# adaLN columns by TensorE with the weights stationary, all of x ahead of the second part, and q and k of a unit in turn

## The reference

```python
cond = jax.nn.silu(c)                                    # (1, 1024)
for i in range(2):
    shift, scale, gate = jnp.split(cond @ w_ada[i] + b_ada[i], 3, axis=-1)
    h = rms_norm(x, g_pre[i]) * (1.0 + scale) + shift    # (1024, 1024)
    u = h @ w_in[i]                                      # q, k, v and z, 1024 columns each
    y = attention_i(u[..., :3072])                       # diff: lambda from exp of two dot products
    y = (y * jax.nn.silu(u[..., 3072:])) @ w_out[i]
    x = x + gate * rms_norm(y, g_post[i])
```

## Time and profile before

| | |
|---|---|
| median of 3 runs | 1553.56 us (1552.69 to 1553.84) |
| the profiled execution | 1552.89 us |
| its span, first to last instruction | 1551.0 us |
| PE busy | 1382.5 us, 89% |
| DVE, ACT, POOL busy | 1057.0, 879.3, 554.8 us |
| mean granted TensorE clock | 0.962 |
| first score matmul of the first layer | at 101.63 us |
| first matmul of z's projection behind it | at 102.15 us |

### The profile page before, as it was taken

The page is one execution under the profiler, slowest core; times in us unless marked ns, Lnnn a source line. Parts: engine busy times, 40 slices in busy tenths (PEclk is TensorE's granted clock), DMA queues, the critical chain, the costliest instruction groups (busy, mean ns, idle before and its releaser), DMA issues. The chain is left out here.

```text
span 1551.0 us, 23600 instructions
## 1 busy us (share of the span) xinstructions
PE 1382.5 (89%) x7154; PEld 1138.9 (73%) x7154; DVE 1057.0 (68%) x1824; ACT 879.3 (57%) x1712; POOL 554.8 (36%) x325
## 2 busy tenths in 40 slices
PE   4688999999999999986997899999999999995898
PEld 2567777777777777775875678887877888784776
DVE  4868888797979797978457656556565656557415
ACT  4346555565656565555445467667676757667322
POOL 1024555555646564636222322121122212122204
PEclk9899999999999999996998899999999999996999
DMA  9012111102021111122034001100100010002014
GB/s 342 28 41 64 46 54 52 56 27 80 28 68 41 54 54 54 54 73 90 1 112 146 28 28 32 37 27 27 41 27 27 27 39 28 27 14 109 0 58 174
DMA packets 112649, 89.82 MB, mean 58 GB/s; under 512 B 2553, under 2 KB 101090, under 8 KB 112610
## 3 DMA queue, kind: packets, MB, share of 16 engines
q1 hardware_dynamic: 112320, 89.15, 18.3%
q10 hardware_dynamic: 290, 0.18, 0.1%
HBM read 80.92 MB, written 8.40 MB: 58 GB/s over the span
## 5 line engine op out<-in xcount | busy, mean ns | idle before, releaser
L674 PE MATMUL bank<-h_hi,w_hi 128*128 128x512 f32 x976 | 396.0, 406 | 9.1 <-POOL h_lo L583 4.5
L674 PE MATMUL bank<-h_lo,w_hi 128*128 128x512 f32 x976 | 393.2, 403 | 0.0
L674 PE MATMUL bank<-h_hi,w_lo 128*128 128x512 f32 x976 | 390.7, 400 | 0.0
L644 POOL TENSOR_TENSOR w_lo<-w_raw,w_hi 128x1024 fp32r<-128x1024 f32 x59 | 159.4, 2701 | 374.6 <-ACT w_hi L638 374.5
L1288 POOL TENSOR_TENSOR a<-a,stick 128x128 f32<-128x128 f32 (+7 forms) x128 | 189.6, 1486 | 251.0 <-DVE stick L1153 251.0
L1153 DVE TENSOR_TENSOR_SCAN stick<-b 128x128 f32<-128x128 f32 (+7 forms) x128 | 204.1, 1594 | 41.4 <-ACT b L1057 41.4
L674 PEld LDWEIGHTS bank<-h_hi,w_hi 128*128 128x128 f32 x976 | 185.9, 190 | 41.6 <-issue 10.0
L674 PEld LDWEIGHTS bank<-h_hi,w_lo 128*128 128x128 f32 x976 | 185.5, 190 | 33.1
L674 PEld LDWEIGHTS bank<-h_lo,w_hi 128*128 128x128 f32 x976 | 185.5, 190 | 30.4
L1056 ACT ACTIVATE a<-bank 128x512 f32<-128x512 f32 (+2 forms) x192 | 94.7, 493 | 90.5 <-PE bank L960 52.6
L1069 ACT ACTIVATE wt_hi<-bank 128x512 fp32r<-128x512 f32 (+2 forms) x192 | 87.8, 494 | 74.8 <-PE bank L976 73.0
(11 more groups left out here) (215 smaller groups left out, 3036.8 us busy)
## 6 DMA issues: line engine op xcount, KB each, us to landing
w_raw<-in_w_in_dram SPq DMA_DIRECT2D x63, 512.0 KB, 4.0
ada_piece<-in_w_ada_dram SPq DMA_DIRECT2D x32, 512.0 KB, 3.8
p_ada<-in_w_ada_dram SPq DMA_DIRECT2D x8, 1024.0 KB, 13.2
wo_raw<-in_w_out_dram SPq DMA_DIRECT2D x8, 1024.0 KB, 9.9
p_x<-in_x_dram SPq DMA_DIRECT2D x8, 512.0 KB, 7.7
o_x<-in_x_dram SPq DMA_DIRECT2D x8, 512.0 KB, 4.1
x_between<-o_res SPq DMA_DIRECT2D x8, 512.0 KB, 2.9
o_x<-x_between SPq DMA_DIRECT2D x8, 512.0 KB, 4.1
```

Source lines behind the costliest of these rows:

```text
L644: self.nc.gpsimd.tensor_tensor(self.m["w_lo"][s][:, :, :], self.m["w_raw"][s][:, :, :], self.m["w_hi"][s][:, :, :].bitcast(F32), ALU.subtr ...
L674: mm = nc.tensor.matmul(self.bank[half][:, :], w[:, k, :], h[:, k, half * HALF:(half + 1) * HALF], start=(i == 0), stop=(i == GROUP - 1))
```

## The change

Parts 0 to 3 are all made by one form on TensorE: for each of 8 blocks of the condition and each of 4 column blocks a matmul with the 128x128 block of w_ada stationary and the condition's column moving, summed in PSUM straight to columns, 32 float32 matmuls a part. The row product, its copy, `accumulate` and the matmuls with ones leave. All eight tiles are normalised and turned before part 1; part 0 stands on TensorE between turns 2 and 3. The tiles' PSUM banks go round in three pairs. Phases 0 and 1 are made in a row, and q and k are projected unit by unit in turn, in phase 2 for the first four of its eight units. Columns 2 and 3 stand where they stood, between v's phases 0 and 1 and phase 2. The loads are ordered accordingly. GpSimd's w_lo is made in four pieces a weight. The Exp of lambda and the three small VectorE instructions on it move to the second layer's start; the loading of the Sigmoid table moves ahead of the last copies. ScalarE's split of z's weights moves behind all six copies of q and k, and VectorE packs one half of q before it takes k.

```diff
-    T = ((0, 1), (6, 7), (0, 1), (6, 7), (6, 7), (4, 1), (6, 7), (4, 1))
+    T = ((0, 1), (6, 7), (3, 4))
...
# sync
         for h in range(2):
             ada(0, h)
-        ada(1, 0)
-        weights(0, self.proj.loaded[0])
-        ada(1, 1)
-        weights(1, self.proj.loaded[1])
         for t in range(4, NT):
             tile(t)
+        weights(0, self.proj.loaded[0])
+        for h in range(2):
+            ada(1, h)
+        weights(1, self.proj.loaded[1])
         weights(2, self.v_loaded)
...
# gpsimd
-            nc.gpsimd.tensor_tensor(self.w_lo[kind][:, :, :], self.w_raw[kind][:, :, :],
-                                    self.w_hi[kind][:, :, :].bitcast(F32), ALU.subtract).then_inc(self.proj.lo_done, 1)
+            for k in range(0, KT, 2):
+                ins = nc.gpsimd.tensor_tensor(self.w_lo[kind][:, k:k + 2, :], self.w_raw[kind][:, k:k + 2, :],
+                                              self.w_hi[kind][:, k:k + 2, :].bitcast(F32), ALU.subtract)
+            ins.then_inc(self.proj.lo_done, 1)
...
# scalar
-        act.wait_ge(self.lam_sum, 2)
-        nc.scalar.activation(self.lam_sums[:, 2:4], self.lam_sums[:, 0:2], ACT.Exp).then_inc(self.lam_exp, 1)
...
+        for t in range(NT):
+            square(t)
+            root(t)
             if t:
                 keep_left(t - 1)
...
+            if t == NT - 1:
+                act.preload_act_table_set("sigmoid_and_others")
+                weights_hi(0, self.proj.loaded[0])
+        keep_left(NT - 1)
         weights_hi(1, self.proj.loaded[1])
...
# vector
+        for t in range(NT):
             normalise(t)
             if t:
                 keep_right(t - 1)
-        keep_right(3)
-        accumulate(1)
+        keep_right(NT - 1)
         columns(0)
...
         modulate(1)
-        accumulate(2)
-        accumulate(3)
         columns(1)
         modulate(2)
...
# tensor
         def columns(i):
             at = (0, KT, self.LOW, KT + self.LOW)[i]
...
+            for k in range(KT):
+                if k % self.LOW == 0:
+                    pe.wait_ge(self.ada_in[i][k // self.LOW], 16)
+                for j in range(self.LOW):
+                    mm = nc.tensor.matmul(self.cols[:, at + j:at + j + 1], self.ada_w[i][:, k, j * P:(j + 1) * P],
+                                          m["cond"][:, k:k + 1], start=(k == 0 and j == 0),
+                                          stop=(k == KT - 1 and j == self.LOW - 1))
+            mm.then_inc(self.cols_done, 1)
...
+        for t in range(NT):
             turn(t)
+            if t == 2:
+                pe.wait_ge(self.cond_done, 1)
+                columns(0)
+        columns(1)
         pe.wait_ge(self.left_kept, NT)
         pe.wait_ge(self.right_kept, NT)
-        for kind in range(2):
-            project(kind, 1)
-        pe.wait_ge(self.proj.lo_done, done(2))
-        project(2, 0)
-        project(2, 1)
-        for i in range(2, 4):
-            columns(i).then_inc(self.cols_done, 1)
+        for phase in range(2):
+            project((0, 1), phase, range(self.LOW))
+        for phase in range(2):
+            project((2,), phase, range(self.LOW))
+        columns(2)
+        columns(3)
+        project((0, 1), 2, range(self.LOW))
         for kind in range(3):
-            project(kind, 2)
+            project((kind,), 2, range(0 if kind == 2 else self.LOW, KT))
...
# behind the prologue: scalar, then vector
             for n in range(6):
                 pack_hi(0, n)
-                if n == 3:
-                    proj.split_hi(act, 0, 3)
+            proj.split_hi(act, 0, 3)
...
-            for n in range(4):
-                pack.lo(dve, 0, n)
+                for n in ((0,), (2, 3, 1))[kind]:
+                    pack.lo(dve, 0, n)
...
# second layer, vector
+            dve.wait_ge(pro.lam_exp, 1)
+            nc.vector.tensor_tensor(lam[:, 0:1], lam[:, 7:8], lam[:, 6:7], ALU.subtract).then_inc(table, 1)
+            dve.wait_ge(table, 5)
+            nc.vector.tensor_scalar(lam[:, 2:3], lam[:, 0:1], -lam_init, None, ALU.add).then_inc(table, 1)
+            nc.vector.tensor_scalar(lam[:, 3:4], lam[:, 1:2], 1.0 - lam_init, None, ALU.mult).then_inc(table, 1)
+            dve.wait_ge(table, 7)
```

More of the change, by code:

```diff
@@ L211, in __init__ @@
         self.vec = m["ada_sum"]
-        self.vec_t, self.row = m["pm"][2], m["pm"][5]
+        self.vec_t = m["pm"][2]
         self.cols = m["pm"][2][:, P:P + 2 * KT]
@@ L311, in statistics, with root @@
                                  accum_out=st[:, 4 * t:4 * t + 1]).then_inc(self.squares, 1)
+        def root(t):
             act.wait_ge(self.mean_done, t + 1)
@@ L378, in keep_right @@
             dve.wait_ge(self.turned, t + 1)
-            t4 = m["pm"][self.T[t][1]][:, :].rearrange("p (k t) -> p k t", t=P)
+            t4 = m["pm"][self.T[t % 3][1]][:, :].rearrange("p (k t) -> p k t", t=P)
             nc.vector.tensor_copy(m["y"][:, 4:8, t * P:(t + 1) * P], t4).then_inc(self.right_kept, 1)
[L382 to L398, removed]
         def columns(batch):
@@ L438, in vector @@
                                            accum_out=self.lam_sums[:, j:j + 1]).then_inc(self.lam_sum, 1)
-        for t in range(4):
+        for t in range(NT):
             normalise(t)
@@ L442, in vector @@
                 keep_right(t - 1)
-        keep_right(3)
-        accumulate(1)
+        keep_right(NT - 1)
         columns(0)
[L446 to L453, removed]
         dve.wait_ge(self.left_kept, NT)
         dve.wait_ge(self.right_kept, NT)
+        modulate(0)
         modulate(1)
-        accumulate(2)
-        accumulate(3)
         columns(1)
         modulate(2)
[L461 to L464, removed]
+        for r in range(2):
+            nc.vector.memset(m["stick"][r][:, S:S + 1], 1.0).then_inc(self.one_set, 1)
     def tensor(self, pe):
@@ L480, in columns @@
             at = (0, KT, self.LOW, KT + self.LOW)[i]
[L481 to L491, removed]
@@ L492, in columns @@
-            return mm
-        def project(kind, phase):
-            units, first = self.units(phase)
[L496 to L506, removed]
+            for k in range(KT):
[5 more added lines that the diff above has]
+                                          stop=(k == KT - 1 and j == self.LOW - 1))
@@ new lines, in columns, with project @@
+            mm.then_inc(self.cols_done, 1)
+        def project(kinds, phase, picked):
+            units, first = self.units(phase)
+            for n in picked:
+                k, half = units[n]
+                pe.wait_ge(self.hi_done, first + n + 1)
+                pe.wait_ge(self.lo_done, first + n + 1)
+                for kind in kinds:
+                    if phase == 0 and n == 0:
+                        pe.wait_ge(self.proj.lo_done, done(kind))
+                    for part in range(MULS):
+                        w = (self.w_hi, self.w_hi, self.w_lo)[part][kind]
+                        h = (m["h_hi"], m["h_lo"], m["h_hi"])[part]
+                        mm = nc.tensor.matmul(m["pm"][self.ACC[kind][half]][:, :], w[:, k, :],
+                                              h[:, k, half * HALF:(half + 1) * HALF],
+                                              start=(k == 0 and part == 0), stop=(k == KT - 1 and part == MULS - 1))
+                    if k == KT - 1:
+                        mm.then_inc(self.proj.group_done, 1)
@@ L1143, in _ @@
             pro.vector(dve)
-            for r in range(2):
-                nc.vector.memset(m["stick"][r][:, S:S + 1], 1.0).then_inc(one_set, 1)
             def scan(p, t):
@@ L1599, in _ @@
             act.preload_act_table_set("natural_log_exp_and_others")
+            act.wait_ge(pro.lam_sum, 2)
+            nc.scalar.activation(m["lam"][:, 6:8], m["lam"][:, 4:6], ACT.Exp).then_inc(pro.lam_exp, 1)
             for kind in range(2):
```

69 lines of the change are left out of this document (18 added, 51 removed).

## The result

| | before | after |
|---|---|---|
| median of the runs | 1553.59 us (1552.69 to 1553.84, 4 runs) | 1581.23 us (1579.23 to 1583.12, 4 runs) |
| the profiled execution, its span | 1552.89 us, 1551.0 us | 1581.02 us, 1579.2 us |
| mean granted clock | 0.962 | 0.952 |
| first matmul of z's projection | 102.15 us | 127.23 us |

The change is slower by 1.8%: the ratio is 1.0179, 95% interval 1.0161 to 1.0196. The forecast of 1581.0 us, slower at 0.90, holds.

What follows compares the result with a forecast made beforehand. TensorE, until its first wide projection matmul of the pair loop, was taken as the bound: that moves from 102.15 to 130.2 us, 28.0 us later, giving 1581.0 us. The range was 1565 to 1586 us, slower at 0.90.

Steps and rivals of the forecast that it cites:

- The decisive price: In the adaLN columns on TensorE: 256 weight loads, 0.213 us each at half clock, 13.7 us a part.
- Rival A: In the columns the clock holds at full, 7.1 us each; not slower, 1550.6 to 1554.4 us; chance 0.10.
- B: In the columns the half clock does not slow loads, only transposes: +4.9 us, 1558 us; chance 0.05.
- Columns 2 and 3: Before phase 2's projections: 128 loads, 2.7 us at full clock and the rest at half, 24.9 us, ending at 105.2.
- Tiles and columns 1: Behind columns 0: turn 7 ends at 45.7 us, then columns 1 all at half clock, 13.7 us, ending at 59.4.
- rival C: Transposes lift the clock again; columns 1 and 2 begin with 4.4 us at full clock: +20.3 us, 1573; chance 0.09.
- the first unit: Between columns 1 and the first projection: VectorE's three links and first unit take 2.7 us, first projection at 62.1.
- From k's end to z: From the last k projection to the pair loop's first: 9.5 us net in place of 10.0, z at 130.2.
- Behind z: From the pair loop's first projection matmul on, everything follows on TensorE and is shifted as it stands.
- With q and k in turn these waits go: In the projections of q and k: q's waits for VectorE's units vanish; the 18.2 us sum has none.
- The small moves: Root of tile 0 2.35 us earlier at the start; k to z 9.5 us, not 10.0; second layer taken as 0.
- Loads: Reordered DMA loads of x, ada and w: bytes unchanged, cover over 15 us in each case, so no waits.

Runs made afterwards that it cites:

- e1: The kernel after with only the first four of the condition's eight blocks in each part, half the weight loads: 1553.21 us.
- e2: The kernel after with the operands of the four parts exchanged, condition stationary and 512 weights moving: 1565.54 us, ratio 1.0085.
- e3: The kernel after with an unused 512-column bfloat16 matmul behind each float32 column matmul: 1576.64 us.
- e5: The kernel after with part 0's columns moved behind turn 7, straight ahead of part 1's: 1583.98 us, ratio 1.0199.
- e6: The kernel e4 with q and k of each phase projected one after another, as in the kernel before: 1544.73 us, ratio 0.9947.
- e7: The kernel before with only the small moves (lambda's Exp, tables, w_lo in four pieces, z's split, packing order): 1550.80 us, ratio 0.9982.
- e4: The kernel after with the old columns: row product for part 0, VectorE's sums for parts 1 to 3: 1546.09 us, ratio 0.9951.
- e8: The kernel e4 with part 0's row product spread between the turns and tiles 4 to 7 loaded ahead of part 1: 1544.90 us, ratio 0.9945.

## Why the prediction was right, and where it was not

| step | predicted | measured |
|---|---|---|
| turn 2 ends | 19.9 | 19.7 |
| columns 0, end | 13.7, 33.6 | 13.65, 33.2 |
| turn 7 ends | 45.7 | 44.3 |
| columns 1, end | 13.7, 59.4 | 12.03, 56.2 |
| first projection | 62.1 | 58.7 |
| projections, end | 18.2, 80.3 | 18.4, 77.2 |
| columns 2 and 3, end | 24.9, 105.2 | 24.67, 101.8 |
| projections to k, end | 12.8, 120.7 | 12.5, 116.7 |
| z | 130.2 | 127.2 |
| z to the end of the span | 1448.8 | 1452.0 |

**The decisive price** held: 256 loads, 0.213 us each at half clock, against a forecast of 0.213; 50.35 us of columns against 52.3. Rival A is out, since the granted clock read 0.50, and B since loads at that clock took 333 ns. The number was partly luck. The prediction had how long a load lasts and needed how far apart two start, and it added the lower end of its rows, 288 ns, without a reason. The loads at half clock then lasted 333 ns, its upper end; worked out its way that is 0.111 + 0.144 = 0.255 us a load and 16.3 us a part. The distance was 0.213 all the same. e1 shows that the number of loads is the cost, e2 and e3 that the half clock belongs to this form. The Trainium skill, "TensorE: Matmul & The Clock Gate", "LDWEIGHTS", gives a load 107 ns at 128 columns and no clock level; the distance in the rows is near it at 1.00 (0.111 to 0.112 us) and about double at 0.50 (0.213). The same page's "Why this matters for your kernels" asks for bursts without long idle gaps; 21.40 of 21.40 us busy at a granted clock of 0.50 is a case where that did not do, and the measurement decides.

**Columns 2 and 3** ran at full clock for 2.9 us behind the wide matmuls (2.7 taken), as the earlier trace rows had shown.

**Tiles and columns 1** came in 3.4 us early in all. By the end of columns 0 it is 0.4 us: TensorE began at 12.64 us and not at the 13.75 implied, but turn 2 took 1.97 us at half clock, which gave most of that back. Turns 3 to 7 took 11.1 us and not 12.1, and turn 7, 1.09 us, was at full clock: half of rival C came true. Columns 1 then had 1.00 for about 2 us, not C's 4.4, which is 1.7 us; the rest is the first unit and rounding. In e5 the turns lifted the clock too, at 21.2 us, but it was at half again for turns 5 to 7, and columns began at 0.213. Why the clock rises among the turns at one point and falls again at another was not settled.

**From k's end to z** the prediction had 9.5 us, and 10.6 were measured, so of the 4.0 us by which k's end came early 1.0 was lost again. The packing gained more than forecast: the first score came 8.25 us behind k's end against 9.51 before. But z stood 2.32 us behind the score and not 0.52, waiting for GpSimd's w_lo (the row of 127.23 above). So the late split of z's weights cost 1.8 us, where the prediction had 1.

**Behind z** is the step that failed: "from there on everything follows on TensorE, and I shift it as it stands". From z to the end of the span took 1451.97 us and not 1448.85, 3.1 us more, and this hid the 3.0 us by which z came early. The two traces, laid side by side instruction by instruction, show where: 0.3 us right behind z, about 0.2 in two spells at half clock that before does not have, 1.0 in small steps over both layers, 1.2 in one burst of the second layer's output projection and 0.4 at the last projection. The spells:

```profile
233.60:237.00 3.40, 3.40 (x11) 2.47 (x10) 3.22 (x4) 1.07 (x3) 3.40 (x3) 0.51 0.00 0
315.60:318.90 3.30, 3.30 (x11) 2.19 (x10) 3.27 (x3) 1.33 (x3) 3.30 (x3) 0.50 0.00 0
```

The burst, in before and then in after:

```profile
1440.50 0.76 PE L825 MATMUL bank<-wo_hi,o_ahead_hi 128*128 128x512 f32 x1 [6.35 <-issue]
...
1443.60 0.39 PE L825 MATMUL bank<-wo_hi,o_ahead_lo 128*128 128x512 f32 x1
...
1447.47 0.39 PE L1411 MATMUL bank<-k_hi,q 128*128 128x512 f32 x1
```
```profile
1467.07 0.77 PE L774 MATMUL bank<-wo_hi,o_ahead_hi 128*128 128x512 f32 x1 [6.78 <-issue]
...
1472.73 0.40 PE L774 MATMUL bank<-wo_hi,o_ahead_lo 128*128 128x512 f32 x1
...
1475.26 0.39 PE L1357 MATMUL bank<-k_hi,q 128*128 128x512 f32 x1
```

The same 24 matmuls took 6.97 us and 8.19 us. In before the clock was back at 1.00 after 7 of them, in after only after 13. It is not a property of the columns: the same distance, worked out as span less z, is 1449.3 us in e6, 1450.3 in e2, 1450.8 in e7, 1450.9 in e1, 1451.9 in e5, 1452.2 in e4, 1452.7 in e3 and 1452.9 in e8, and e4 and e8 have the old columns. The order is that of the moment at which the clock comes back in this burst, from 1341.4 us behind z in before and 1341.8 in e6 to 1345.4 in after and 1346.3 in e8; only e3 stands out of line (1343.4), and it has 6.8 us at half clock at the last projection where the others have 3.4. Part of that order is only that a delay from earlier moves both. These are single profiled executions, and what sets the moment stays open. The sum of the prediction, right to 0.1 us, owes that to two errors of 3 us against each other.

**"With q and k in turn these waits go"** was right of the rows and worth nothing in the time of the kernel: e6, where the packing takes back part of what the projections gain. **The small moves** I took at 2.35 us at the start and 0.5 us at k; e7 measured 2.8 us of z together, 3.5 us at the start and a part of it lost again behind. **All of x ahead** would be worth the rest of the 9.3 us that e4 gains, 6.5 us; that is a difference, no run has it alone. **Loads**: no projection or column of after waited for a DMA, as argued.

## What to carry to other kernels

Count weight loads before moving a matrix-vector product onto TensorE: with the matrix stationary and one column moving, each 128x128 block of float32 cost two loads, here 0.213 us each at the half clock that this form itself ran at, so 13.7 us for a whole 1024x512 part, against 7 to 9 us as a row product and little for sums on VectorE that lie under wide matmuls (TensorE waited 1.89 us for the last of them in e4, but 5.96 us in e8, where nothing lay over one). Busy time is no proof of progress; read the granted clock of the stretch beside it. When a change of many parts loses, keep the order and put back the one part that costs: here that gave 1544.7 to 1546.1 us (e4, e6, e8), faster than either kernel.

## What was unexpected in the hardware

- Added work made a stretch shorter: a 512-column bfloat16 matmul between the one-column float32 ones took the granted clock from 0.50 to 1.00; a pair of loads with it takes 0.353 us, against 0.426 us without (e3).
- Transposes alone lifted the clock and did not hold it: in e5, with nothing else on TensorE, the granted clock rose to 1.00 at 21.2 us (turn 4, 1.09 us) and fell back at 24.6 (turns 5 to 7, 1.97 us each). In after turn 7 ran at 1.00 (1.09 us).
- GpSimd's subtraction in pieces of 128x256 slows VectorE's beside it from 0.69 us to between 1.04 and 1.24 us (e4), and in e8 six of its sums took 6.87 us, 1.15 us each, against 0.744 in the earlier trace rows, beside eight such pieces (30.87 to 39.77 us). The Trainium skill, "SBUF — State Buffer", "SBUF: two separate sides", says that GpSimd and an instruction of VectorE with two inputs in SBUF lock a shared pair of ports against each other for whole instructions; these rows, whose VectorE instructions have two such inputs, agree with that in direction. They show that VectorE still waits when GpSimd's instructions are cut in four.
